# A two-layer encoder step on one core: full-row stick-breaking scores, value turn and late evictions moved, small moves in the down projection

## The chip, the core and the metric

One NeuronCore of a Trainium2 chip runs the whole program as one launch. The metric is the device time of one execution in microseconds (us). The engines work side by side, each with its own queue of instructions, and wait for each other by semaphores: TensorE (PE; its weight loads are shown as PEld), VectorE (DVE), ScalarE (ACT), GpSimd (POOL), and SyncE (SP), which issues most of the DMAs.

## The reference, cut to what matters

One inference step of a trunk with two layers for two requests at once: a prompt of 512 tokens and a sample of 64 tokens that has 512 cached keys. Layer 0 mixes tokens by attention with forget gates, layer 1 by stick-breaking attention; both have 12 heads of 64 and, beside them, 4 heads that read 256 memory tokens.

```python
def sb_block(q, k, v, qpos, kpos):
    z = jnp.einsum('bqhd,bkhd->bhqk', q.astype(jnp.float32), k.astype(jnp.float32)) * SCALE
    mask = kpos[None, :] < qpos[:, None]
    u = jnp.where(mask, jax.nn.log_sigmoid(-z), 0.0)
    rest = lax.cumsum(u, axis=3, reverse=True) - u
    a = jnp.where(mask, jnp.exp(jax.nn.log_sigmoid(z) + rest), 0.0)
    return jnp.einsum('bhqk,bkhd->bqhd', a.astype(v.dtype), v)
...
    x = x + o @ w_out
    gate, up = jnp.split(rmsnorm(x, g_ffn) @ w_gate_up, 2, axis=-1)
    return x + (jax.nn.silu(gate) * up) @ w_down
```

D_MODEL is 1024, D_FF 2816. Everything is fp32.

## The kernel before

Activations lie with features on the 128 partitions and the 576 tokens (64 of the sample, then 512 of the prompt) along the free axis. A large product is made of three products in a faster fp32 format: each operand is split into a high half (made by ACT) and a low half (the rest, by VectorE or GpSimd), and high x high, high x low and low x high are added (`passes`, L692). A weight tile of 512 KB is loaded by SP (`slab`, L428), gets its high half from ACT (`high`, L1010) and its low half from GpSimd (`low`, L567), and is then used by TensorE in eight pieces of six matmuls.

Attention goes by calls: two memory calls and six pair calls (two heads each) in each layer (`calls`). A call has nine units: for each of four blocks of 128 queries one for each head (units 0 to 7), and unit 8 for the sample's 64 queries of both heads. TensorE's order in a call is written out by hand in `attention` (L851): in every unit some pieces of the input projection for a later pair (`fill`, shared out by `spread`), the transposes of the unit before (`turn`, into the PSUM bank `turned`, from which ACT copies), and the scores of a unit further on. The products with the values of the call before stand in unit 0 (`values`, prompt) and unit 3 (`values_sample`). The value tile of the call's own pair is turned in unit 1, between two pieces (L884). In the last call the pieces are those of the output projection.

ACT and VectorE run the same units in their own `attention` (L1149, L1466). A forgetting unit goes VectorE (`front`), ACT (exponential), VectorE (`normalize`); a stick-breaking unit goes ACT (`softplus`, three activations), VectorE (`front`: a sum, a reversed scan, a difference), ACT (exponential). Between, ACT copies what was turned, makes the high halves of the finished outputs (`out_high`) and of a weight tile; VectorE makes their low halves (`out_low`, tile `o_lo`) and takes finished projections out of PSUM (`fill_out`). `out_ps`, one PSUM bank, is free again for the late sample product only when `out_low(prev, 0)` is done.

In `scores_one` (L774) a stick score contracts the 64 rows of one head: head 0 on partitions 0 to 63, head 1 on 64 to 127, and the mask is added by a product of 128 rows after it. The sample scores (L785) contract all 128 rows, with queries that are zero in the other head's rows.

The down projection (`down`, L959) makes each pair of output tiles from seven products (a scheme with block sums) in three chunks of the hidden features. Per product ACT makes the weight's high half (`d_high`) and, for five of seven, a copy of the weight in PSUM; VectorE makes the low half from the copy, or from SBUF where there is none (`d_copy`, `d_low`), and adds the product to x. In a layer's last chunk ACT also splits the new x (`split_new`), VectorE makes x's low half in layer 0, GpSimd adds the squares.

Of the kernel before, what the change touches and what calls it, by code (L numbers as in the profile page):

```python
# [99 lines left out]
def build(nc, x_t, mem_t, w_mkv, w_in, w_f, w_out, w_gu, w_dn, gains, b_f, ck, cv, clf, cmk, cmv,  # L100
# [4 lines left out]
    def sb(name, shape, dt=F32, stack=ctx):  # L105
# [40 lines left out]

    gates = at("gates", [P, 2, 2, SEQ])
    ckb = [gates[:, i] for i in range(2)]
    ckbs_cum = at("ckbs_cum", [P, 2 * KEYS_S])
    ckbs = [ckbs_cum[:, i * KEYS_S:(i + 1) * KEYS_S] for i in range(2)]  # L150
# [14 lines left out]
    m_lo = [sb("m_lo", [P, KT, N_MEM], F32R, region)[:, :, :],  # L165
            gates[:, :, :, :].bitcast(F32R).rearrange("p a b (k c) -> p (a b k) c", c=N_MEM)]
    region.close()
# [126 lines left out]
    class Call:  # L294
# [4 lines left out]

        def __init__(self, layer, half, par, mem=False, tiles=(), spread=(0,) * UNITS, fill=0):  # L300
            self.layer, self.par, self.mem = layer, par, mem
            self.a = a = half * 2 + par
            self.last = isinstance(a, int) and a == ATTNS - 1
            self.stick = layer == 1 and not mem
            self.pair = None if mem else a - MEM_PAIRS
            self.o_tile = PAIRS + a if mem else a - MEM_PAIRS
            self.unit = (a + layer * ATTNS) * UNITS
            self.use = attn_use(layer, a)
            start = 2 * DEPTH + layer * LAYER_ROUNDS
            self.round = a * MEM_ROUNDS + start if mem else \  # L310
                a * PAIR_ROUNDS + (start + MEM_PAIRS * (MEM_ROUNDS - PAIR_ROUNDS))
            self.out = (a + layer * ATTNS) * 2
            self.qkv = layer * IN_TILES + a + 1 if mem else a * 3 + (layer * IN_TILES - 1)
            self.qk = self.qkv if mem else self.qkv - 1
            self.caches = (half + (layer * ATTNS // 2 + 1)) * 32
            self.cums = half * 64
            self.tiles = tiles
            self.slabs = [fill * 6 + (layer_slab(layer) + t) for t, _ in tiles]
            self.nums = [fill * 6 + (layer_tile(layer) + t) for t, _ in tiles]
            self.spread = spread  # L320

            beside = [u for u, n in enumerate(spread) for _ in range(n)]
            self.per = len(beside) // len(tiles) if tiles else 0
            self.starts = [beside[self.per * n] for n in range(len(tiles))] if beside else []
            self.ends = [beside[self.per * n + self.per - 1] for n in range(len(tiles))] if beside else []
# [32 lines left out]
    def calls(eng, layer, call):  # L358
# [4 lines left out]
        def pair(half, par, t, fill=0):  # L363
            return Call(layer, half, par, False, [(t + c, "qkv"[c]) for c in range(3)],
                        (2, 2, 2, 3, 3, 3, 3, 3, 3) if layer else (1, 3, 3, 3, 2, 3, 2, 3, 4), fill)

# [3 lines left out]
        last = Call(layer, ATTNS // 2 - 1, 1, False, [(IN_TILES, "o"), (IN_TILES + 1, "o")],  # L370
                    (0, 1, 2, 1, 1, 0, 0, 1, 1) + (1,) * 7)
        call(mem0, None, mem1)
# [36 lines left out]
    def d_copy(pair, p):  # L409

        n = pair * PRODUCTS + p % PRODUCTS
        return acc[:, n // 2 % 2, n % 2, :] if p >= RING and p % PRODUCTS not in (1, 4) else None

# [152 lines left out]
    def _(pool):  # L566
# [16 lines left out]
        def zero_rows(layer):  # L583


            tiles = [vf_z[:, 0:DEC]]
            for par in range(2):
                tiles += [qs[par][HD:P, 0:DEC], qs[par][0:HD, DEC:]]
            for n, tile in enumerate(tiles):
                pool.memset(tile, 0.0).then_inc(zeroed, 1)  # L590
                pool.wait_ge(zeroed, len(tiles) * layer + n + 1)

# [98 lines left out]
    def _(pe):  # L691
# [82 lines left out]
        def scores_one(c, u):  # L774

            i, hd = divmod(u, 2)
            if u == 0:
                pe.wait_ge(qkv_ready, c.qk)
            pe.wait_ge(score_free, c.use + u - 1)
            rows, out = slice(hd * HD, (hd + 1) * HD), score[:, c.buf(u), 0:c.width(u)]  # L780
            pe.matmul(out, q[c.par][rows, DEC + i * P:DEC + (i + 1) * P], kb[c.par][rows, KEYS_S:KEYS_S + c.width(u)],  # L781
                      start=True, stop=False)
            mask_on(c, u, out).then_inc(score_ready, 1)
# [67 lines left out]
        def attention(c, prev, nxt):  # L851
# [24 lines left out]
            for u in range(UNITS):  # L876
                pieces = c.spread[u]
                half = pieces // 2
                fill(pieces - half)
                if u == 0 and prev is not None:  # L880
                    turn(prev, 2 * QT)
                    values(prev)
                    turn_rest(prev)
                if u == 1 and not c.mem:  # L884
                    pe.wait_ge(qkv_ready, c.qkv)
                    turn_blocks(c.round, vf[:, DEC:], QT)
                if u == 3 and prev is not None:
                    values_sample(prev)
                fill(half)
                if u:  # L890
# [29 lines left out]
        for layer in range(DEPTH):  # L920
# [19 lines left out]
            product(s0 + 1, t0 + 1, 1, 1, xg_hi, xg_lo)  # L940
            pe.wait_ge(zeroed, 5 * (layer + 1))
            pe.wait_ge(masks_made, 1)
# [66 lines left out]
    def _(act):  # L1009
# [139 lines left out]
        def attention(c, prev, nxt):  # L1149
            if prev is None and c.stick:  # L1150
                softplus(c, 0)
            for u in range(UNITS):
# [7 lines left out]
                if u == 1 and prev is not None:  # L1160
                    out_high(prev, 0)
                if u == 1 and not c.mem:
                    copy_round(c.round, v[c.par][:, :, :], turned[:, :].rearrange("p (j c) -> p j c", j=QT))
                if u:
                    copy_turned(c, u - 1)
                if u == 4 and prev is not None:
                    out_high(prev, 1)
# [18 lines left out]
        for layer in range(DEPTH):  # L1186
# [83 lines left out]
            for chunk, count in enumerate(CHUNKS):  # L1270
# [9 lines left out]
                for p in range(CHUNK_PRODUCTS):  # L1280
                    if p + RING < CHUNK_PRODUCTS:
                        d_high(chunk, p + RING)
                    if p < 3:
                        tail_high(chunk, p + 2)
                    if p == PRODUCTS and (chunk < len(CHUNKS) - 1 or layer < DEPTH - 1):
                        high(sg + 2 * (CHUNK0[chunk] + count) + 1, 1)
                    m, r = divmod(p, PRODUCTS)
                    if chunk == len(CHUNKS) - 1:
                        if r == 6:
                            split_new(2 * m)  # L1290
                        elif r == 0 and m:
                            split_new(2 * m - 1)
# [6 lines left out]
    def _(dve):  # L1299
# [62 lines left out]

        def queries(slab, tpar, par, scale):
            dve.wait_ge(slab_done, slab + 1)
            for hd in range(2):
                rows, cols = slice(hd * HD, (hd + 1) * HD), slice(hd * DEC, (hd + 1) * DEC)
                dve.scalar_tensor_tensor(out=qs[par][rows, cols], in0=acc[rows, tpar, 0, 0:DEC], scalar=scale,
                                         in1=rstd[rows, 0:DEC], op0=ALU.mult, op1=ALU.mult)
            return tile_out(slab, tpar, [(q[par], slice(0, P), scale)])

# [63 lines left out]
        def fill_out(c, n):  # L1434
# [3 lines left out]
            if what == "q":  # L1438
                last = queries(slab, t % 2, par, -SCALE if c.layer == 0 else SCALE)
            elif what == "k":  # L1440
# [12 lines left out]
        def attention(c, prev, nxt):  # L1453
            if prev is None:
                front(c, 0)
            for u in range(UNITS):
# [8 lines left out]
                if not c.stick and not early:  # L1465
                    normalize(c, u)  # L1466
                if u in (2, 5) and prev is not None:
                    out_low(prev, u // 5)
                if u in c.ends and c.tiles[0][1] != "o":
# [260 lines left out]
```

## Time and profile before

| | us |
|---|---|
| median of 3 runs (1481.46 to 1485.0) | 1483.07 |
| profiled execution | 1484.24 |
| its span | 1482.5 |
| granted TensorE clock, mean | 0.994 |
| PE busy | 1421.3 (96%) |
| DVE busy | 852.0 (57%) |
| ACT busy | 684.6 (46%) |
| POOL busy | 528.7 (36%) |

Busy time is the time in which an engine has an instruction under way; for TensorE it holds overlaps and ends that are modelled. Of the chain of work that ended last, 86% is TensorE's, 6% ACT's, 5% VectorE's. The times of the rows below are us from the start of the span.

### The profile page before, as it was taken

Reading aid. Unit: us, or ns where it says so; the run is one execution under the profiler, and the core shown is the slowest. Engines: PE = TensorE matmul, PEld = TensorE weight load, DVE = VectorE, ACT = ScalarE, POOL = GpSimd, SP = SyncE. Lnnn points to the kernel's source line nnn. Section 1 sums busy time; section 2 is a strip of 40 time slices with the busy share of each in tenths; the row PEclk is TensorE's granted clock in tenths of the full one; section 3 lists DMA queues with packets and bytes.
Section 4 is the critical chain, followed back from the end, with each engine's and each line's share of the span. In section 5 each row is a group of like instructions: output and inputs, shape, how many; then the busy total and the mean of one; then the engine's idle time right before and its main releaser. Section 6 shows DMA issues by size and latency. Waiting matters only on the chain.

```text
span 1482.5 us, 25893 instructions
## 1 busy us (share of the span) xinstructions
PE 1421.3 (96%) x10248; PEld 1321.6 (89%) x10248; DVE 852.0 (57%) x1376; ACT 684.6 (46%) x1287; POOL 528.7 (36%) x291
## 2 busy tenths in 40 slices
PE   6899999899999999999899999989999999999995
PEld 5778888699999999999887777758999999999995
DVE  6655555424574566456755655663257555755575
ACT  5454444533362236224745667674424422532364
POOL 2511212064433354334632111113534334433444
PEclk9999999999999999999999999999999999999998
DMA  6233333122322232223222222211223223222222
GB/s 260 74 95 126 117 110 111 41 75 86 115 71 72 85 106 79 71 85 107 64 72 88 76 77 81 74 45 44 85 86 97 75 85 113 72 72 85 99 59 92
DMA packets 49438, 130.69 MB, mean 88 GB/s; under 512 B 5532, under 2 KB 11676, under 8 KB 49216
## 3 DMA queue, kind: packets, MB, share of 16 engines
q1 hardware_dynamic: 44688, 121.23, 24.7%
q10 hardware_dynamic: 4656, 8.21, 1.5%
q8 instruction: 58, 0.95, 0.3%
q14 instruction: 36, 0.29, 0.1%
HBM read 118.85 MB, written 10.57 MB: 87 GB/s over the span
## 4 chain that ended last, share of the span: by engine, by line
PE 86%; ACT 6%; DVE 5%; issue 1%; DVEq 0%; DMA 0%; ACTq 0%; POOL 0%; SPq 0%; POOLq 0%
PE acc L699 60%; PE score L983 8%; PE out_ps L983 4%; PE turned L804 3%; PE out_ps L833 2%; PE score L781 2%; PE turned L983 2%; PE score L766 1%; ACT w_hi L1019 1%; DVE d_lo L1578 1%; PE out_ps L844 1%; PE score L793 1%; PE score L754 1%; DVE work_b L1416 1%; ACT work_c L1043 0%
## 5 line engine op out<-in xcount | busy, mean ns | idle before, releaser
L571 POOL TENSOR_TENSOR w_lo<-w_raw,w_hi 128x1024 fp32r<-128x1024 f32 x142 | 344.7, 2428 | 673.2 <-ACT w_hi L1019 651.9
L699 PE MATMUL acc<-xg_hi,w_hi 128*128 128x288 f32 x2048 | 452.1, 302 | 0.8 <-POOL w_lo L571 0.8
L699 PE MATMUL acc<-xg_hi,w_lo 128*128 128x288 f32 x2048 | 438.3, 296 | 0.0
L699 PE MATMUL acc<-xg_lo,w_hi 128*128 128x288 f32 x2048 | 438.0, 295 | 0.0
L699 PEld LDWEIGHTS acc<-xg_hi,w_hi 128*128 128x128 f32 x2048 | 327.8, 189 | 8.7 <-issue 7.1
L699 PEld LDWEIGHTS acc<-xg_hi,w_lo 128*128 128x128 f32 x2048 | 329.5, 188 | 0.0
L699 PEld LDWEIGHTS acc<-xg_lo,w_hi 128*128 128x128 f32 x2048 | 329.2, 188 | 0.0
L1019 ACT ACTIVATE w_hi<-w_raw 128x1024 fp32r<-128x1024 f32 x146 | 154.4, 1058 | 363.7 <-PE acc L699 356.5
L1531 DVE TENSOR_TENSOR work_b<-work_b,rstd 128x576 f32<-128x576 f32 x44 | 94.4, 2146 | 39.5 <-ACT work_b L1221 39.5
L983 PE MATMUL score<-f_hi,d_hi 128*128 128x288 f32 x352 | 105.0, 298 | 6.9 <-DVE x L1587 6.8
L1118 ACT ACTIVATE pt<-turned 128x256 f32<-128x256 f32 (+3 forms) x128 | 53.8, 420 | 115.7 <-PE turned L804 114.6
L983 PE MATMUL score<-f_lo,d_hi 128*128 128x288 f32 x352 | 103.8, 295 | 0.0
L983 PE MATMUL score<-f_hi,d_lo 128*128 128x288 f32 x352 | 103.7, 295 | 0.0
L580 POOL TENSOR_TENSOR sumsq<-sumsq,work_c 128x576 f32<-128x576 f32 x34 | 50.7, 1491 | 127.9 <-ACT work_c L1043 127.6
L1557 DVE TENSOR_TENSOR f_lo<-f_new,f_hi 128x576 fp32r<-128x576 f32 (+1 forms) x38 | 73.2, 1925 | 40.2 <-ACT f_hi L1232 40.2
L1578 DVE TENSOR_TENSOR d_lo<-acc,d_hi 128x512 fp32r<-128x512 f32 (+1 forms) x108 | 69.5, 644 | 40.5 <-ACT d_hi L1257 40.2
L804 PE MATMUL turned<-cst,work_b 128*128 128x128 f32 x372 | 68.3, 278 | 13.2 <-ACT vs L1118 5.3
L1357 DVE TENSOR_TENSOR work_a<-acc,rstd 128x576 f32<-128x576 f32 x44 | 33.2, 755 | 75.5 <-PE acc L699 62.1
L1545 DVE TENSOR_TENSOR f_new<-acc,work_b 128x576 f32<-128x576 f32 x38 | 28.8, 757 | 82.4 <-PE acc L699 82.4
L983 PEld LDWEIGHTS score<-f_hi,d_hi 128*128 128x128 f32 x352 | 66.0, 187 | 9.6 <-DVE d_lo L1578 7.6
L1383 DVE SCALAR_TENSOR_TENSOR work_a<-score,work_c 128x512 f32<-128x512 f32 (+3 forms) x54 | 27.7, 514 | 69.7 <-ACT work_c L1104 67.0
L804 PEld LDWEIGHTS turned<-cst,work_b 128*128 128x128 f32 x372 | 46.5, 141 | 22.3 <-issue 11.2
(181 smaller groups left out, 2429.8 us busy)
## 6 DMA issues: line engine op xcount, KB each, us to landing
w_raw<-in_w_gu SPq DMA_DIRECT2D x88, 512.0 KB, 3.4
w_raw<-in_w_in SPq DMA_DIRECT2D x40, 512.0 KB, 3.5
w_raw<-in_w_out SPq DMA_DIRECT2D x16, 512.0 KB, 3.5
d_raw<-in_w_dn SPq DMA_DIRECT2D x16, 512.0 KB, 3.7
d_raw<-in_w_dn SPq DMA_DIRECT2D x32, 256.0 KB, 2.7
out_k_o<-kb ACTq DMA_DIRECT2D x12, 288.0 KB, 2.5
out_v_o<-vf_z ACTq DMA_DIRECT2D x12, 288.0 KB, 3.2
kb<-in_ck SPq DMA_DIRECT2D x12, 256.0 KB, 2.6
```

The source lines that it names most:

```text
L571: pool.tensor_tensor(w_lo[par][:, 0:cols], raw(s, par, cols), w_hi[par][:, 0:cols].bitcast(F32), ALU.subtract).then_inc(wlo_made, 1)
L580: pool.tensor_tensor(sumsq[:, :], sumsq[:, :], work_c[:, m % 2, :], ALU.add) \
L699: mm = pe.matmul(acc[:, tpar, h, 0:c1 - c0], w[par][:, k * P:(k + 1) * P], a[:, c0:c1], start=first and n == 0, stop=last and n == 2)
L781: pe.matmul(out, q[c.par][rows, DEC + i * P:DEC + (i + 1) * P], kb[c.par][rows, KEYS_S:KEYS_S + c.width(u)], start=True, stop=False)
L804: mm = pe.transpose(turned[:, j * P:(j + 1) * P], tile[:, j * P:(j + 1) * P], ident)
L983: mm = pe.matmul(bank, w, a[:, f, k, :], start=(k == 0 and q == 0 and r in (0, 1, 3)), stop=(k == kts - 1 and q == 2), skip_group_check=True)
L1019: act.activation(w_hi[par][:, 0:cols], raw(s, par, cols), ACT.Copy).then_inc(whi_made, 1)
L1118: act.activation(out, src, ACT.Copy).then_inc(turned_free, 1)
L1357: last = dve.tensor_tensor(halves(out), src, halves(rstd[rows, :]), ALU.mult)
L1531: dve.tensor_tensor(work_b[:, 0, :], work_b[:, 0, :], rstd[:, :], ALU.mult)
L1557: dve.tensor_tensor(f_lo[:, own, i, :], src, f_hi[:, own, i, :].bitcast(F32), ALU.subtract) .then_inc(flo_made, 1)
L1578: dve.tensor_tensor(d_lo[:, n % RING, 0:cols], whole[:, 0:cols], d_hi[:, n % RING, 0:cols].bitcast(F32), ALU.subtract).then_inc(dlo_made, 1)
```

## The change

- `scores_one` reads queries from a new tile `qz`: for each head 128 rows, of which the other head's 64 are zero; the matmul takes all 128 rows of the keys. In layer 1 `queries` writes each head's 64 rows there, in two instructions, in place of the one to `q`; four memsets on GpSimd at the start of layer 1 zero the rest. `qz` lies where the forget gates lay; the low half of the second layer's memory tile gets a name of its own at the same place.
- The value tile is turned in unit 0, after that unit's pieces, in place of unit 1; ACT's copy of it moves likewise.
- In pair calls other than the last, all pieces of units 1 to 8 come before the late sample product and the turn. In layer 0 one piece moves from unit 8 to unit 0.
- In the last call the late sample product moves from unit 3 to 2, its `out_high` from 4 to 2, the two `out_low` from units 2 and 5 to 1 and 3.
- In the down projection the high half of the weight tile that follows a chunk moves four products later; half of the splits of x move two products later; in layer 0's last chunk, behind the first pair, the two products without a PSUM copy are 2 and 5 in place of 1 and 4.

```diff
+    early = ExitStack()
+    m_lo1 = sb("m_lo1", [P, KT, N_MEM], F32R, early)
+    early.close()
+    gate_room = at("gate_room", [P, 2 * 2 * SEQ + 2 * KEYS_S])
+    qz = gate_room[:, 0:2 * 2 * TOK].rearrange("p (a b c) -> p a b c", a=2, b=2)
...
+            self.late = (2, 2, 1, 3) if last else (3, 4, 2, 5)
...
-                        (2, 2, 2, 3, 3, 3, 3, 3, 3) if layer else (1, 3, 3, 3, 2, 3, 2, 3, 4), fill)
+                        (2, 2, 2, 3, 3, 3, 3, 3, 3) if layer else (2, 3, 3, 3, 2, 3, 2, 3, 3), fill)
...
-        return acc[:, n // 2 % 2, n % 2, :] if p >= RING and p % PRODUCTS not in (1, 4) else None
+        beside_x = pair // OUT_PAIRS == len(CHUNKS) - 1 and p > PRODUCTS
+        return acc[:, n // 2 % 2, n % 2, :] if p >= RING and p % PRODUCTS not in ((2, 5) if beside_x else (1, 4)) else None
...
                 tiles += [qs[par][HD:P, 0:DEC], qs[par][0:HD, DEC:]]
+                if layer:
+                    tiles += [qz[HD:P, par, 0, :], qz[0:HD, par, 1, :]]
...
-            rows, out = slice(hd * HD, (hd + 1) * HD), score[:, c.buf(u), 0:c.width(u)]
-            pe.matmul(out, q[c.par][rows, DEC + i * P:DEC + (i + 1) * P], kb[c.par][rows, KEYS_S:KEYS_S + c.width(u)],
+            out = score[:, c.buf(u), 0:c.width(u)]
+            pe.matmul(out, qz[:, c.par, hd, DEC + i * P:DEC + (i + 1) * P], kb[c.par][:, KEYS_S:KEYS_S + c.width(u)],
...
-                half = pieces // 2
+                half = pieces // 2 if u == 0 or c.last or c.mem else 0
                 fill(pieces - half)
...
-                if u == 1 and not c.mem:
+                if prev is not None and u == c.late[0]:
+                    values_sample(prev)
+                fill(half)
+                if u == 0 and not c.mem:
                     pe.wait_ge(qkv_ready, c.qkv)
                     turn_blocks(c.round, vf[:, DEC:], QT)
-                if u == 3 and prev is not None:
-                    values_sample(prev)
-                fill(half)
...
-            pe.wait_ge(zeroed, 5 * (layer + 1))
+            pe.wait_ge(zeroed, (5, 14)[layer])
...
-                if u == 1 and not c.mem:
+                if u == 0 and not c.mem:
                     copy_round(c.round, v[c.par][:, :, :], turned[:, :].rearrange("p (j c) -> p j c", j=QT))
...
-                if u == 4 and prev is not None:
+                if prev is not None and u == c.late[1]:
                     out_high(prev, 1)
...
-                    if p == PRODUCTS and (chunk < len(CHUNKS) - 1 or layer < DEPTH - 1):
+                    if p == PRODUCTS + 4 and (chunk < len(CHUNKS) - 1 or layer < DEPTH - 1):
                         high(sg + 2 * (CHUNK0[chunk] + count) + 1, 1)
...
-                        elif r == 0 and m:
+                        elif r == 2 and m:
                             split_new(2 * m - 1)
...
+            if stick:
+                return tile_out(slab, tpar, [(qz[hd * HD:(hd + 1) * HD, par, hd, :], slice(hd * HD, (hd + 1) * HD), scale)
+                                             for hd in range(2)])
...
-                if u in (2, 5) and prev is not None:
-                    out_low(prev, u // 5)
+                if prev is not None and u in c.late[2:]:
+                    out_low(prev, c.late[2:].index(u))
```

## Rows read from the trace of the kernel before

**Rows 1.** The page, busy us, share of the span and instructions of each engine.
```profile
PE 1421.3 (96%) x10248; PEld 1321.6 (89%) x10248; DVE 852.0 (57%) x1376; ACT 684.6 (46%) x1287; POOL 528.7 (36%) x291
```

**Rows 2.** Busy us by stretch: stretch, length, each engine, PEclk, DMA share, GB/s.
```profile
198.79:230.22 31.43, 31.43 (x230) 26.76 (x229) 17.51 (x47) 13.98 (x36) 7.16 (x3) 1.00 0.36 113
904.36:939.91 35.55, 34.92 (x230) 27.91 (x229) 21.29 (x37) 24.87 (x56) 7.18 (x3) 1.00 0.22 77
...
995.00:1000.00 5.00, 3.06 (x8) 1.64 (x8) 4.52 (x8) 2.95 (x6) 0.00 (x0) 0.50 0.00 0
```

**Rows 3.** Waits of PE from 760 to 1013: us in total, times, longest.
```profile
PE turned L804 <- ACT vs L1118: 4.5, 6, 1.4
...
PE out_ps L844 <- DVE o_lo L1424: 1.8, 2, 1.0
```

**Rows 4.** Order of time, PE, a 64-row stick score: start, us, what, count.
```profile
886.81 0.38 PE L804 MATMUL turned<-cst,work_b 128*128 128x128 f32 x2
887.12 1.12 PE L781 MATMUL score<-kb,qb 64*128 64x512 f32 x2
...
888.56 0.42 PE L699 MATMUL acc<-xg_lo,w_hi 128*128 128x288 f32 x2
```

**Rows 5.** Order of time, PE, the 128-row sample score of the same call.
```profile
894.67 0.49 PE L804 MATMUL turned<-cst,work_b 128*128 128x128 f32 x3
...
895.86 0.33 PE L793 MATMUL out_ps<-kb,qs 128*128 128x64 f32 x2
896.03 0.19 PE L754 MATMUL out_ps<-mask_b,ident_b 128*128 128x64 bf16 x1
...
896.41 0.43 PE L699 MATMUL acc<-xg_lo,w_hi 128*128 128x288 f32 x2
```

**Rows 6.** Order of time, PEld, the weight loads of that sample score.
```profile
894.89 0.30 PEld L793 LDWEIGHTS score<-kb,qs 128*128 128x128 f32 x2
```

**Rows 7.** Order of time, ACT, units 0 and 1 of a stick-breaking pair call.
```profile
907.20 1.05 ACT L1019 ACTIVATE w_hi<-w_raw 128x1024 fp32r<-128x1024 f32 x1
...
910.55 0.59 ACT L1118 ACTIVATE vs<-turned 128x512 f32<-128x512 f32 x1
```

**Rows 8.** Order of time, PE, unit 3 of that call.
```profile
916.19 0.42 PE L699 MATMUL acc<-xg_lo,w_hi 128*128 128x288 f32 x2
916.45 0.43 PE L699 MATMUL acc<-xg_hi,w_lo 128*128 128x288 f32 x2
916.73 1.13 PE L844 MATMUL out_ps<-pts,vcs 128*128 128x128 f32 x8
```

**Rows 9.** Order of time, DVE, the end of the sample unit of that call.
```profile
937.36 0.21 DVE L1390 TENSOR_TENSOR work_a<-out_ps,work_c 128x64 f32<-128x64 f32 x1
```

**Rows 10.** Order of time, PE, unit 6 of layer 1's last call; idle before in brackets.
```profile
997.86 2.05 PE L793 MATMUL score<-kb,qs 128*128 128x512 f32 x2 [1.74 <-DVE o_lo L1430]
```

**Rows 11.** Order of time, PE, unit 3 of layer 0's last call.
```profile
272.38 1.13 PE L844 MATMUL out_ps<-pts,vcs 128*128 128x128 f32 x8 [1.18 <-DVE o_lo L1424]
```

**Rows 12.** Order of time, PE, the fifth product in both layers' last chunk.
```profile
715.88 0.37 PE L983 MATMUL score<-f_hi,d_hi 128*128 128x288 f32 x1 [1.82 <-DVE x L1587]
728.27 0.37 PE L983 MATMUL score<-f_hi,d_hi 128*128 128x288 f32 x1 [0.96 <-DVE x L1587]
...
1450.03 0.37 PE L983 MATMUL score<-f_hi,d_hi 128*128 128x288 f32 x1 [0.87 <-DVE x L1587]
```

**Rows 13.** Order of time, ACT, before the first of these waits.
```profile
711.04 1.04 ACT L1019 ACTIVATE w_hi<-w_raw 128x1024 fp32r<-128x1024 f32 x1
```

**Rows 14.** Line L1578, low halves read from SBUF: ns min/median/max, first and last start, forms.
```profile
L1578 DVE TENSOR_TENSOR d_lo<-d_sum,d_hi x54: 542/681/1955, 403.3 to 1459.0; 128x512 fp32r<-128x512 f32 x36, 128x384 fp32r<-128x384 f32 x18
```

**Rows 15.** Order of time, DVE, a pair's queries.
```profile
919.89 0.76 DVE L1359 SCALAR_TENSOR_TENSOR qb<-acc,rstd 128x576 f32<-128x576 f32 x1
```

**Rows 16.** Order of time, POOL, the start of layer 1.
```profile
749.61 0.75 POOL L590 MEMSET qs<- 64x64 f32 x4
753.53 2.41 POOL L571 TENSOR_TENSOR w_lo<-w_raw,w_hi 128x1024 fp32r<-128x1024 f32 x1 [3.17 <-ACT w_hi L1019]
```

More of the change, by code:

```diff
@@ L145, in build @@
     pts = at("pts", [P, QT * P + P])
-    gates = at("gates", [P, 2, 2, SEQ])
+    early = ExitStack()
+    m_lo1 = sb("m_lo1", [P, KT, N_MEM], F32R, early)
+    early.close()
+    gate_room = at("gate_room", [P, 2 * 2 * SEQ + 2 * KEYS_S])
+    gates = gate_room[:, 0:2 * 2 * SEQ].rearrange("p (a b c) -> p a b c", a=2, b=2)
     ckb = [gates[:, i] for i in range(2)]
-    ckbs_cum = at("ckbs_cum", [P, 2 * KEYS_S])
+    ckbs_cum = gate_room[:, 2 * 2 * SEQ:]
+    qz = gate_room[:, 0:2 * 2 * TOK].rearrange("p (a b c) -> p a b c", a=2, b=2)
     ckbs = [ckbs_cum[:, i * KEYS_S:(i + 1) * KEYS_S] for i in range(2)]
@@ L165, in build @@
     m_lo = [sb("m_lo", [P, KT, N_MEM], F32R, region)[:, :, :],
-            gates[:, :, :, :].bitcast(F32R).rearrange("p a b (k c) -> p (a b k) c", c=N_MEM)]
+            m_lo1[:, :, :]]
     region.close()
@@ L294, in build, with __init__ @@
     class Call:
-        def __init__(self, layer, half, par, mem=False, tiles=(), spread=(0,) * UNITS, fill=0):
+        def __init__(self, layer, half, par, mem=False, tiles=(), spread=(0,) * UNITS, fill=0, last=False):
             self.layer, self.par, self.mem = layer, par, mem
@@ L370, in calls @@
         last = Call(layer, ATTNS // 2 - 1, 1, False, [(IN_TILES, "o"), (IN_TILES + 1, "o")],
-                    (0, 1, 2, 1, 1, 0, 0, 1, 1) + (1,) * 7)
+                    (0, 1, 2, 1, 1, 0, 0, 1, 1) + (1,) * 7, last=True)
         call(mem0, None, mem1)
@@ L588, in zero_rows @@
                 tiles += [qs[par][HD:P, 0:DEC], qs[par][0:HD, DEC:]]
+                if layer:
+                    tiles += [qz[HD:P, par, 0, :], qz[0:HD, par, 1, :]]
             for n, tile in enumerate(tiles):
                 pool.memset(tile, 0.0).then_inc(zeroed, 1)
-                pool.wait_ge(zeroed, len(tiles) * layer + n + 1)
+                pool.wait_ge(zeroed, 5 * layer + n + 1)
         for n in range(2):
@@ L1361, in tile_out, with queries @@
             return last
-        def queries(slab, tpar, par, scale):
+        def queries(slab, tpar, par, scale, stick=False):
             dve.wait_ge(slab_done, slab + 1)
+            if stick:
+                dve.wait_ge(zeroed, 14)
             for hd in range(2):
@@ L1368, in queries @@
                                          in1=rstd[rows, 0:DEC], op0=ALU.mult, op1=ALU.mult)
+            if stick:
+                return tile_out(slab, tpar, [(qz[hd * HD:(hd + 1) * HD, par, hd, :], slice(hd * HD, (hd + 1) * HD), scale)
+                                             for hd in range(2)])
             return tile_out(slab, tpar, [(q[par], slice(0, P), scale)])
@@ L1438, in fill_out @@
             if what == "q":
-                last = queries(slab, t % 2, par, -SCALE if c.layer == 0 else SCALE)
+                last = queries(slab, t % 2, par, -SCALE if c.layer == 0 else SCALE, c.layer == 1)
             elif what == "k":
```

## The prediction

> **What bounds the kernel now.** I read the page first: TensorE is busy 96% of the span [rows 1]. Then the busy times call by call. A call of layer 0 is full of TensorE work, 31.43 of 31.43 us; a stick-breaking call of layer 1 takes 35.55 with 34.92 busy, while ACT works 24.87 and VectorE 21.29 [rows 2]. So TensorE's queue is the bound, and a change pays by taking time out of it or by removing a wait in it. The waits of TensorE in layer 1 say which there are: on ACT's copy of the turned value tile (`vs`, 4.5 us in six waits, the longest 1.4 in the last call, so 0.62 in each of the other five) and on VectorE's `o_lo` (1.8 in two, 0.8 and 1.0) [rows 3]. "Busy" also hides something, which only the order of time shows: next part.
>
> **The scores.** Take a 512-column stick score, 64 rows deep. The transposes before it end at 886.81 + 0.38 = 887.19, and the input projection runs evenly again from 888.56: 1.37 us [rows 4]. The sample score of the same call does the same with 128 rows: transposes end at 895.16, even running from 896.41, 1.25 us, and in it are 0.17 of a second small product (896.03 - 895.86) and a mask narrower by 64 columns, about 0.03 [rows 5]. Without them 1.11. The two 512-column products themselves are not faster or slower by rows; the difference is at the two ends, where TensorE goes from full to half rows and back. Price: 0.26 us a score. There are 6 pairs x 8 = 48 of them: 2 beside the second memory call, 8 beside each of five pair calls, 6 in the last. That is 12.5 us of TensorE's queue, at most.
>
> The weights of the 128-row score begin to load at 894.89, while the transposes still run [rows 6]. The Trainium skill, "TensorE: Matmul & The Clock Gate", The mechanism, says that a weight load overlaps a running matmul only where the row groups differ; full-row scores would then pay for their loads. The row says otherwise, so I give that rule a small chance as a rival below.
>
> **Value turn, u = 1 to u = 0.** The five waits of 0.62 go, since the copy of the value tile is now a unit ahead of the turn that waits for it. What is late next is ACT. Before, ACT did a weight copy (1.05) and went straight to the softplus of unit 2; the value copy (0.59) came a unit later [rows 7]. Now the value copy waits for the value turn behind TensorE's second piece, the weight copy comes after it, and softplus 2 starts some 1.1 us later, while TensorE comes earlier. From it hang unit 2's and 3's VectorE work and then `o_lo`, for which the late sample product waits: now it starts at 916.73 with one piece (0.79: three pairs of matmuls, 0.26 apart) still to come [rows 8]. ACT reaches softplus 3 about when it does now (what it has to do before that is the same, in another order), so `o_lo` and that product come about where they are, at 916.6 by my count, but with the piece done: 0.9 us won, where 3 scores and the value wait would be worth 1.4. I book 0.6 handed back (with the little wait there). At the end of a call the next call's second score needs the buffer that VectorE frees when the sample unit is done, at 937.57 [rows 9]; TensorE comes to it only a little after that, and by one or two scores (0.26 to 0.52) sooner after the change: 0.2 handed back. The call that waited 0.8 for `o_lo` loses that too, as all three pieces now come before.
> Five pair calls: 5 x (8 x 0.26 + 0.62) + 0.8 - 5 x 0.8 = 10.3.
>
> **Last calls.** In layer 1 it is a chain, not a queue: ACT, VectorE and TensorE wait for each other, and the sample scores start at 997.86 after 1.74 of idling [rows 10]. Following ACT's order: the value turn first costs a wait of half a us, as no piece covers it; its 1.4 wait goes; the sample product a unit earlier lets VectorE's `o_lo` out of the way before unit 6. I get the sample scores at about 995.8, 2.0 earlier, with the second memory call's two scores (0.5, of which 0.2 handed back) 2.3. TensorE is granted half its clock there (0.50, the 1.2 GHz level, in 995 to 1000, in which it is busy 3.06 of 5.00) [rows 2]; I leave that as it is. In layer 0 the last call waits 1.18 for `o_lo` [rows 11]; the same move takes that wait, lets the units behind it start sooner, and delays one pair of scores by a us: 1.5 gained.
>
> **Layer 0's other calls.** No wait to remove, and one more piece at u = 0, one less at u = 8, are the same pieces. Value: 0, bounds -1.5 to +1.5.
>
> **Down projection.** In each layer's last chunk TensorE stands before the fifth product of a pair: 1.82, 0.96, 0.96 in layer 0, 0.42 and 0.87 in layer 1, together 5.0 [rows 12]. ACT is the cause: it does x's split, and in layer 0's second pair a weight copy of 1.04 too, before the high half that this product needs [rows 13]. The change puts the copy four products later and the split two; both fit between other high halves there. What may be late next is VectorE: the low halves that are read from SBUF alone move to the two products beside which x's low half is made, and such a low half takes 0.68 alone and up to 1.96 [rows 14]. I take 4.0 of the 5.0, bounds 2.5 and 5.0. The Trainium skill, "SBUF — State Buffer", Who interferes with whom, has VectorE with two SBUF inputs shut out for a whole GpSimd instruction; by it a pair could give back another us, 3 less in all.
>
> **What is added.** Two half-height products for the padded query in place of one: 0.76 more on VectorE for each pair [rows 15], 4.6 in all, hidden by its 14 us of idling in a call [rows 2]; uncovered it would cost those 4.6. Four memsets of 576 columns on GpSimd: no row; from 0.2 each (as those of 64 columns, 0.19 apart) to 1.8 (in proportion), I take 0.2, the nearest row. GpSimd idles 3.17 before its next weight half [rows 16]; even 7.2 in all would delay that half (from 753.53, 2.41 long) by 4.0, to 760.0, when TensorE needs it. SP's cache loads are released by the late sample product, now 0.7 later within its unit in most calls; the weight tile queued behind them is copied three units (11 us) later. Nothing.
>
> **Sum.** 10.3 + 2.3 + 1.5 + 4.0 = 18.1. The profiled execution took 1484.24 (span 1482.5); 1484.2 - 18.1 = 1466.1. The median of the runs is 1.2 below the profiled one: 1465.0.
>
> **Rivals.**
> - *ACT hands most of it back.* If softplus 2's lateness runs through the whole call, a pair call gains 1.0 instead of 2.1, the last ones 1.5 together, the down projection 2.5: 9.0, so 1474. For it: ACT is without slack around units 0 and 1; against: 10.7 us of idling in a call [rows 2].
> - *Nothing is handed back.* 14.3 in the pair calls, 0.5 beside the memory call, the last calls 4.5 and 3.0 (the clock stays up), down 5.0: 27.3, so 1456. Against it is ACT's order, worked out above.
> - *The padding does nothing*, because the time at the ends belongs to the mask or the scores themselves: only waits go, 3.9 + 1.0 + 1.5 + 4.0 = 10.4, 1473. Against it: [rows 4, 5].
> - *Full-row loads are not hidden* (the skill's rule above): two loads of 0.19 against 0.26 saved, 48 x 0.12 = 5.8 lost, other gains 10.4: 1478. Against it: [rows 6].
> - *Slower.* The call starts become the bound in both layers: softplus 2 later by the weight copy (1.05) in six calls, layer 0's second pair of scores later by a piece and the turn (1.3) in six, nothing won on the scores: 6.3 + 7.8 - 4.0 in the down projection, 1493. It decides only where the chain from those scores has less than 1.3 us in hand when its turn is due; layer 0's calls show no wait at all [rows 2].
>
> **Chances.** Forecast 0.56, most handed back 0.18, nothing handed back 0.13, padding does nothing 0.06, loads 0.02, slower 0.05. About 0.2% (3 us) can be told from no change. Faster: all but the last, less 0.03 for a first rival that hands back the rest as well: 0.92; same 0.03; slower 0.05. Range 1457 to 1475: it leaves out the far ends of the second and the last rival.
>
> **What would show it.** After an L781 score no gap of its load, and even running 1.1 us after the transposes; the line `turned <- ACT vs` gone from TensorE's waits; pair calls of about 33.5; the softplus of unit 2 later against its score; the last chunk's waits before the fifth product below 0.4. Wrong if pair calls stay above 34.5, or if TensorE shows new waits on ACT's copies at u = 0 or 1 in layer 0.

## The result and the profile after

The changed kernel takes 1461.73 us (median of 4 runs, 1461.07 to 1461.87) against 1483.53 for the kernel before, timed beside it: ratio 0.985, 95% interval 0.9838 to 0.9863. Forecast were 1465.0, and 1457 to 1475 as the range. The time fell into the range; of the terms of the sum the largest came out over a third larger than forecast, and another less than half of its forecast. The profiled execution took 1461.77 (span 1460.0), 22.5 less than that of before.

TensorE's busy time fell by 15.3 us and its share stayed [rows 1]:

```profile
PE 1406.0 (96%) x10248; PEld 1322.6 (91%) x10248; DVE 857.3 (59%) x1382; ACT 681.4 (47%) x1287; POOL 529.4 (36%) x295
```

A call is measured from its first matmul with the values to that of the next call. Busy times of the calls that answer to [rows 2], of layer 1's last call, and of the stretch in it with the low clock (stretch, length, PE, PEld, DVE, ACT, POOL, PEclk, DMA share, GB/s):

```profile
198.19:229.46 31.27, 31.27 (x231) 26.73 (x230) 17.51 (x47) 13.98 (x36) 7.16 (x3) 1.00 0.34 113
889.25:922.03 32.78, 32.66 (x230) 28.22 (x229) 21.60 (x38) 24.23 (x56) 7.19 (x3) 1.00 0.24 83
954.82:987.51 32.69, 24.69 (x140) 17.84 (x139) 17.99 (x30) 21.44 (x49) 2.37 (x1) 0.90 0.10 35
972.82:978.82 6.00, 4.63 (x9) 2.02 (x10) 4.24 (x6) 4.17 (x8) 0.00 (x0) 0.54 0.00 1
```

The pair call of layer 1 went from 35.55 to 32.78, and one of layer 0, which was to stay, lost 0.16. All calls put against those of before give this table (us, read from the two traces; the row of the down projections holds all that lies behind a layer's last call):

| term of the sum | forecast | measured |
|---|---|---|
| five pair calls of layer 1 | 10.3 | 14.3 |
| second memory call's two scores and layer 1's last call | 2.3 | 0.9 (0.17 + 0.76) |
| layer 0's last call | 1.5 | 1.3 |
| layer 0's other calls | 0 | 0.7 (four by 0.17) |
| down projections | 4.0 | 5.0 (3.5 + 1.5) |
| before the first call | – | 0.3 |
| sum | 18.1 | 22.5 |

The sum was 4.4 too small: 6.0 too little in four rows, of which 1.6 too much in the two rows of the last calls hid a part. That the total came as near as it did is in so far luck.

**The scores** did what was forecast. The same stretch as in [rows 4], first TensorE, then its weight load:

```profile
909.10 0.49 PE L816 MATMUL turned<-cst,work_b 128*128 128x128 f32 x3
909.43 1.02 PE L793 MATMUL score<-kb,gate_room 128*128 128x512 f32 x2
910.29 0.22 PE L766 MATMUL score<-mask_b,ident_b 128*128 128x128 bf16 x1
...
910.67 0.42 PE L711 MATMUL acc<-xg_lo,w_hi 128*128 128x288 f32 x2
```

```profile
909.32 0.30 PEld L793 LDWEIGHTS score<-kb,gate_room 128*128 128x128 f32 x2
909.86 0.10 PEld L766 LDWEIGHTS score<-mask_b,ident_b 128*128 128x128 bf16 x1 [0.24 <-issue]
```

From the end of the transposes (909.10 + 0.49 = 909.59) to even running (910.67) are 1.08 us; 1.37 before. The load of the full-row score begins at 909.32, inside the transposes.

**ACT, units 0 and 1**, the rows that answer to [rows 7], with the softplus of units 2 (894.58) and 3 (896.82):

```profile
893.14 0.60 ACT L1130 ACTIVATE vs<-turned 128x512 f32<-128x512 f32 x1 [0.95 <-PE turned L816]
893.63 1.05 ACT L1031 ACTIVATE w_hi<-w_raw 128x1024 fp32r<-128x1024 f32 x1
894.58 0.37 ACT L1111 ACTIVATE work_c<-score 128x256 f32<-128x256 f32 x1
...
896.82 0.39 ACT L1111 ACTIVATE work_c<-score 128x256 f32<-128x256 f32 x1
```

Softplus 2 is late, as forecast: its score was complete at 893.6, 1 us before. From 850 to 954, three pair calls but for the last 0.8 us, TensorE's waits have no line any more; in those 0.8 us the last pair call has a wait of 0.70 on ACT (at 954.26). The order of time shows what that view leaves out, here VectorE's front of unit 2 and then TensorE:

```profile
897.29 0.42 DVE L1407 TENSOR_TENSOR work_a<-score,work_c 128x256 f32<-128x256 f32 x1
```

```profile
897.42 0.27 PE L816 MATMUL turned<-cst,work_b 128*128 128x128 f32 x1
897.82 0.91 PE L793 MATMUL score<-kb,gate_room 128*128 128x384 f32 x2
...
901.06 0.94 PE L856 MATMUL out_ps<-pts,vcs 128*128 128x128 f32 x7
```

The score of unit 4 starts when that front has freed its buffer, 0.40 behind the transpose's start, in place of 0.11 where nothing is waited for (run 5 below). The late sample product at 901.06 waits for nothing.

**Layer 1's last call** (954.82 to 987.51) now waits in other places:

```profile
PE score L793 <- DVEq L1409: 2.6, 2, 1.3
PE turned L816 <- ACT pt L1130: 2.1, 2, 1.2
PE out_ps L856 <- DVE o_lo L1441: 1.8, 1, 1.8
PE score L805 <- DVEq L1409: 1.1, 1, 1.1
PE turned L816 <- ACT pts L1130: 0.5, 1, 0.5
```

### The profile page after: what moved, and what is told of

It reads as the page before. It is cut to its first block, busy times and chain, and to the rows that moved or that the text cites. A ratio compares the mean times of both kernels' runs of the same rounds, so it can differ in the third digit from the quotient of the medians.

```text
span 1460.0 us, 25909 instructions
## 1 busy us (share of the span) xinstructions
PE 1406.0 (96%) x10248; PEld 1322.6 (91%) x10248; DVE 857.3 (59%) x1382; ACT 681.4 (47%) x1287; POOL 529.4 (36%) x295
## 4 chain that ended last, share of the span: by engine, by line
PE 88%; DVE 5%; ACT 4%; issue 1%; DVEq 1%; DMA 0%; POOL 0%; ACTq 0%; SPq 0%; POOLq 0%
PE acc L711 60%; PE score L995 9%; PE out_ps L995 4%; PE turned L816 3%; PE out_ps L845 2%; PE turned L995 2%; PE score L778 2%; PE score L793 1%; ACT w_hi L1031 1%; PE score L805 1%; PE out_ps L856 1%; DVE work_c L1403 1%; DVE work_b L1433 1%; PE score L766 0%; DMA m_raw<-in_mem_t 0%
## 5 line engine op out<-in xcount | busy, mean ns | idle before, releaser
L590 POOL TENSOR_TENSOR sumsq<-sumsq,work_c 128x576 f32<-128x576 f32 x34 | 50.2, 1475 | 134.5 <-ACT work_c L1055 134.4
L1433 DVE TENSOR_SCALAR work_b<-work_b,inv 128x256 f32<-128x256 f32 (+4 forms) x90 | 62.3, 693 | 8.1 <-issue 0.9
L995 PEld LDWEIGHTS score<-f_hi,d_lo 128*128 128x128 f32 x352 | 66.2, 188 | 0.0
```

Of the source, the lines that this page charges most:

```text
L590: pool.tensor_tensor(sumsq[:, :], sumsq[:, :], work_c[:, m % 2, :], ALU.add) \
L995: mm = pe.matmul(bank, w, a[:, f, k, :], start=(k == 0 and q == 0 and r in (0, 1, 3)), stop=(k == kts - 1 and q == 2), skip_group_check=True)
L1433: dve.tensor_scalar(work_b[:, b, 0:w], work_b[:, b, 0:w], inv[:, b:b + 1], None, ALU.mult).then_inc(probs_ready, 1)
```

## Experiments

Nine kernels; the first four were timed together, the next four too, the last by itself, each time beside the kernel before (1483.33, 1483.79, 1482.74). The ratio is to the kernel before. Runs 5 and 6 lie 1.7 us below the changed kernel, and their intervals overlap with its own; what they tell rests on the traces.

| | median us | ratio, 95% interval |
|---|---|---|
| scores on 64 rows again | 1471.70 | 0.9918 (0.9904 to 0.9932) |
| value turn back | 1467.50 | 0.9892 (0.9876 to 0.9908) |
| down projection back | 1467.27 | 0.9894 (0.9878 to 0.9909) |
| before, padding alone | 1476.02 | 0.9950 (0.9936 to 0.9964) |
| weight copy first | 1460.03 | 0.9836 (0.9823 to 0.9850) |
| last call: value turn at unit 1 | 1460.06 | 0.9836 (0.9822 to 0.9849) |
| last call rearranged | 1458.09 | 0.9823 (0.9809 to 0.9836) |
| weight first and last call | 1455.78 | 0.9810 (0.9796 to 0.9823) |
| the same, scores on 64 rows | 1468.48 | 0.9899 (0.9876 to 0.9923) |

**1. Scores on 64 rows again.**

```diff
-            pe.matmul(out, qz[:, c.par, hd, ...], kb[c.par][:, ...],
+            pe.matmul(out, qz[rows, c.par, hd, ...], kb[c.par][rows, ...],
```

> The changed kernel with one thing undone: a stick-breaking score reads the 64 rows of its own head again instead of all 128 (the zero halves are still written, but not read). Theory A (a 64-row score between 128-row matmuls costs TensorE's queue 0.26 us, 48 times, and nothing of it is handed back): 12.5 us more, 1474.2, a pair call of layer 1 2.1 longer (34.9 instead of 32.8). Rival B (ACT or VectorE takes back a part, as forecast: about 0.8 of 2.1 in a call): 1470, a pair call 34.1. Rival C (the padding does nothing, the gain came from the waits and the order): 1461.7.

10.0 more, a pair call 34.64. The same stretch, and the call:

```profile
915.98 0.49 PE L816 MATMUL turned<-cst,work_b 128*128 128x128 f32 x3
916.40 1.12 PE L793 MATMUL score<-kb,gate_room 64*128 64x512 f32 x2
917.45 0.23 PE L766 MATMUL score<-mask_b,ident_b 128*128 128x128 bf16 x1
...
917.84 0.42 PE L711 MATMUL acc<-xg_lo,w_hi 128*128 128x288 f32 x2
```

```profile
895.00:929.64 34.64, 34.64 (x230) 27.88 (x229) 21.71 (x38) 24.54 (x56) 7.22 (x3) 1.00 0.23 79
```

From 916.47 (915.98 + 0.49) to 917.84 are 1.37 again, with nothing changed but the rows: rival C falls. A call loses 1.86, between A and B: something is handed back in the changed kernel, but not 0.8. And the moves alone, without the padding, are worth 35.55 - 34.64 = 0.91 a call, where the wait that they removed was read as 0.62.

The weight loads show where the price of a score lies:

```profile
916.40 0.29 PEld L793 LDWEIGHTS score<-kb,gate_room 64*128 64x128 f32 x2 [0.17 <-issue]
917.45 0.10 PEld L766 LDWEIGHTS score<-mask_b,ident_b 128*128 128x128 bf16 x1 [0.76 <-issue]
```

Between products that all take 128 rows a load begins under the product before: in the changed kernel 0.11 ahead of its score (909.32 for 909.43) and 0.43 ahead of its mask (909.86 for 910.29). Where the rows change it begins only with its own product, here at 916.40 and 917.45, and so in all 48 scores of this run. From start to start this makes 0.09 more before the score, 0.10 more in the first of its two passes (the x2), 0.09 more before the mask and 0.01 behind it: 0.30 a score, at 128 columns as at 512. Whether the load itself or something that holds it up takes the time, the records do not tell.

**2. Value turn back at unit 1.**

```diff
-                half = pieces // 2 if u == 0 or c.last or c.mem else 0
+                half = pieces // 2
...
-                if u == 0 and not c.mem:
+                if u == 1 and not c.mem:
                     pe.wait_ge(qkv_ready, c.qkv)
                     turn_blocks(c.round, vf[:, DEC:], QT)
...
```

> The changed kernel with the value turn back at unit 1, on TensorE and ACT, and the pieces of the input projection in their old places. Theory A (the move is worth the waits that it took away: 0.62 in each of five pair calls of layer 1, up to 1.0 in its last call, 0.17 in four calls of layer 0, and the wait of 0.8 for o_lo): 3.8 to 5.6 more, 1465.5 to 1467.3, and the line of waits on ACT's vs is there again. Rival B (ACT's lateness at softplus 2 handed back what the wait gave, as forecast 0.6 in a call): about 1 more, 1462.7. Rival C (with the scores shorter the chain behind the turn decides, so the wait grows by what the scores gave): 8 or more, 1470.

5.8 more. Waits of TensorE over three pair calls (850 to 961), then a pair call and layer 1's last call:

```profile
PE turned L816 <- ACT vs L1130: 1.9, 3, 0.6
PE out_ps L856 <- DVE o_lo L1441: 1.4, 3, 0.5
```

```profile
893.84:927.75 33.91, 32.83 (x231) 28.22 (x230) 21.59 (x38) 24.48 (x56) 7.18 (x3) 1.00 0.24 80
961.66:993.33 31.67, 25.58 (x140) 19.06 (x139) 17.96 (x30) 21.54 (x49) 2.38 (x1) 0.84 0.10 36
```

A pair call takes 1.13 more, theory A by place, with a wait on top that A did not have: `o_lo` is now late in every call. Layer 0's calls are back at 31.43, so the 0.17 there belong to this move, with the pieces that go along with it. Layer 1's last call, against all theories, is 1.0 *shorter* than in the changed kernel: there the move costs.

**3. Down projection back.**

```diff
-        beside_x = pair // OUT_PAIRS == len(CHUNKS) - 1 and p > PRODUCTS
+        beside_x = False
...
-                    if p == PRODUCTS + 4 and (chunk ...
+                    if p == PRODUCTS and (chunk ...
...
-                        elif r == 2 and m:
+                        elif r == 0 and m:
```

> The changed kernel with the three moves in the down projection undone. Theory A (the five waits before the fifth product were all of it, and VectorE's low halves cost nothing in their new place): 5.0 more, 1466.7. Rival B (a fifth to a half of it is handed back by the low halves that are now made beside x's): 2.5 to 4.0 more, 1464.2 to 1465.7, and waits of TensorE for them in the changed kernel that are gone here.

5.5 more by the runs, 5.0 by the traces (3.7 in layer 0, 1.4 in layer 1). TensorE's waits for x in layer 0's last chunk, here and then in the changed kernel:

```profile
PE score L995 <- DVE x L1604: 3.9, 4, 1.8
```

```profile
PE score L995 <- DVE x L1604: 0.5, 1, 0.5
```

Theory A but for one wait: a fifth product is waited for no more, and the one wait that is left in the changed kernel, 0.45, is rival B's. TensorE comes to a third product that waits for VectorE's sum, which stands behind a low half of 1.42 beside GpSimd:

```profile
717.36 1.80 POOL L662 TENSOR_TENSOR d_sum<-d_raw 128x512 f32<-128x512 f32 x1 [1.06 <-DVE d_lo L1595]
718.29 1.42 DVE L1595 TENSOR_TENSOR d_lo<-d_sum,d_hi 128x512 fp32r<-128x512 f32 x1
720.22 0.37 PE L995 MATMUL score<-f_hi,d_hi 128*128 128x288 f32 x1 [0.45 <-DVE x L1604]
```

The longest of the low halves read from SBUF is now 1.43 where [rows 14] has 1.96. Which of the three moves took which wait was not tried.

**4. The kernel before with the padding alone** (the changed kernel with the edits of runs 2 and 3 together, and `late` at (3, 4, 2, 5) in every call).

> The kernel before with the padded queries alone: value turn, late evictions, pieces and down projection as before. Theory A (the padding is worth 0.26 on the queue at each of 48 scores whatever else is done): 12.5 less than the 1483.5 of before, 1471.0, and the waits on vs and o_lo stay as they are. Rival B (without the moves the chain over ACT and VectorE keeps its time, so TensorE comes earlier to the same waits: vs and o_lo grow by about 0.8 in a call): 8.5 less, 1475. Rival C: the padding does nothing, 1483.

7.3 less: rival B, and more of it than B said. A pair call takes 33.92 in place of 35.55, 1.63 less. Waits over three pair calls (850 to 960):

```profile
PE turned L816 <- ACT vs L1130: 1.9, 3, 0.6
PE out_ps L856 <- DVE o_lo L1441: 1.4, 3, 0.5
```

The wait on `vs` did not grow; the one on `o_lo`, which [rows 3] have in one of these three calls, is now in all three. So the padding by itself does hand back some 0.6 a call, at the place that the prediction named, and the value turn's move takes that away again.

**5. Weight copy first.** In unit 0 ACT makes the weight's high half (`weight` holds the lines that stood further down) before the copy of the value tile, not after it.

```diff
+                if u == 0 and u in c.starts:
+                    weight()
                 if u == 0 and not c.mem:
                     copy_round(c.round, v[c.par]...
...
-                if u in c.starts:
+                if u and u in c.starts:
```

> The changed kernel with ACT's order at unit 0 of a call turned round: first the weight copy, which waits for nothing, and then the copy of the value tile, for which ACT now stands 0.95 us. Theory A (what a pair call of layer 1 hands back is ACT's lateness at the softplus of unit 2: TensorE's score of unit 4 starts 0.38 late, behind VectorE's front of unit 2, in each call): softplus 2 starts 0.9 sooner, the 0.38 goes in five calls, a pair call 32.4, the time 1459.8. Rival B (that wait hangs on something else, VectorE's own queue for one): 32.8 and 1461.7. Rival C (the value copy, 0.6 later, is now late for TensorE's turn of unit 0): new waits on vs, 1463 or more.

1.7 less than the changed kernel. ACT, then TensorE at the score of unit 4, and the call:

```profile
891.14 1.06 ACT L1031 ACTIVATE w_hi<-w_raw 128x1024 fp32r<-128x1024 f32 x1
892.19 0.60 ACT L1130 ACTIVATE vs<-turned 128x512 f32<-128x512 f32 x1
892.68 0.38 ACT L1111 ACTIVATE work_c<-score 128x256 f32<-128x256 f32 x1
```

```profile
896.47 0.27 PE L816 MATMUL turned<-cst,work_b 128*128 128x128 f32 x1
896.58 0.81 PE L793 MATMUL score<-kb,gate_room 128*128 128x384 f32 x2
```

```profile
888.30:920.71 32.41, 32.41 (x230) 28.21 (x229) 21.60 (x38) 24.40 (x56) 7.18 (x3) 1.00 0.24 84
```

Theory A, in place and size: ACT's 0.95 of idling is filled, softplus 2 starts 4.38 into the call in place of 5.33, the score follows its transpose by 0.11, the call is 0.37 shorter. What a pair call handed back was ACT's lateness, and it was 0.37.

**6. Value turn at unit 1 in layer 1's last call alone.**

```diff
+            self.turn_at = 1 if last and layer else 0
...
-                if u == 0 and not c.mem:
+                if u == c.turn_at and not c.mem:
```

> The changed kernel with the value turn back at unit 1 in the last call of layer 1 alone. Theory A (in that call the forecast 2.0 failed because the value turn at unit 0, which no piece covers, holds up ACT and so o_lo, and the sample product waits 1.75 for it): the 1.75 goes, 1.4 on vs comes back, the chain behind it starts 1.0 sooner; the last call 31.7 instead of 32.7, the time 1460.7. Rival B (the end of that call hangs on VectorE's and ACT's chain alone, whatever the turn does): 32.7, 1461.7.

1.7 less. The last call, and in it the turn that waits on `vs` and the late sample product:

```profile
955.19:985.73 30.54, 23.27 (x141) 17.82 (x140) 17.98 (x30) 21.67 (x49) 2.37 (x1) 0.94 0.11 38
```

```profile
961.02 0.30 PE L817 MATMUL turned<-cst,work_b 128*128 128x128 f32 x1 [1.43 <-ACT vs L1134]
...
962.60 1.05 PE L857 MATMUL out_ps<-pts,vcs 128*128 128x128 f32 x8
...
976.23 1.10 PE L806 MATMUL score<-kb,qs 128*128 128x512 f32 x2 [1.95 <-DVEq L1413]
```

Theory A: the 1.75 on `o_lo` is gone, 1.43 on `vs` is back, and the sample scores start 21.04 into the call in place of 22.07 (976.89 - 954.82). The trace shows 2.15 less, not 1.0: the call is, instruction for instruction, that of run 2, where it took 31.67 with its sample scores at the same 21.05; the 1.1 between them lie behind that point. There the granted clock differs (the call's mean is 0.94 here and 0.84 in run 2): the first two passes of the sample score, to the next product, took 0.93 here (976.23 to 977.16) and 1.84 in run 2 (982.71 to 984.55), at the 1.2 GHz level.

**7. Layer 1's last call rearranged.**

```diff
+            self.late = (3, 3, 1, 4) if last and layer else (2, 2, 1, 3) if last else (3, 4, 2, 5)
+            if last and layer:
+                self.starts = [5] + self.starts[1:]
...
-                    (0, 1, 2, 1, 1, 0, 0, 1, 1) + (1,) * 7, last=True)
+                    ((0, 1, 1, 1, 1, 1, 1, 1, 0) if layer else (0, 1, 2, 1, 1, 0, 0, 1, 1)) + (1,) * 7, last=True)
```

> As the run with the value turn back at unit 1 in layer 1's last call, and in that call besides: the late sample product back at unit 3 with its o_lo still made at unit 1 and 4, the output projection's pieces one each at units 1 to 7 (units 5 and 6, where TensorE waits 1.3, get one each), and the weight copy at unit 5 instead of unit 1, out of the way of the softplus of unit 3. Theory A (the call is one chain of score, softplus and VectorE's front, two buffers deep, and it runs as early as its first links: score 4 comes 1.7 sooner, softplus 3 0.8 sooner): the last call 29.5 to 30, the time 1458.5 to 1459. Rival B (the links behind it, on VectorE 2.8 and on ACT 3.1 a unit, set the pace from the start): 31.7, 1460.7. Rival C (the sample product at unit 3 delays the later scores instead): over 32.7, over 1461.7.

3.6 less than the changed kernel, the call 29.27. Theory A: the score of unit 4 starts 7.52 into the call and the sample scores 19.57, so what comes early in that chain keeps most of its lead to the end. How the gain is shared between the sample product, the pieces and the weight copy was not tried.

**8. Weight copy first and the rearranged last call.**

> The weight copy first at unit 0 and the rearranged last call of layer 1 together. If both hold: 1461.7 less 1.9 less 2.7 to 3.2, 1456.6 to 1457.1; if only the weight copy holds 1459.8, if only the last call 1458.7.

5.9 less than the changed kernel; its interval to the kernel before (0.9796 to 0.9823) lies wholly below that of the changed kernel, so it beats both. By the traces 1.9 of it lie in the five pair calls and 3.6 in the last call. Its last call, with the score of unit 4 and the sample scores (the changed kernel has them 10.46 and 22.07 into the call, here 7.52 and 19.58):

```profile
952.47:981.54 29.07, 21.89 (x140) 16.50 (x139) 17.98 (x30) 21.32 (x49) 2.36 (x1) 1.00 0.11 39
```

```profile
959.99 0.81 PE L796 MATMUL score<-kb,gate_room 128*128 128x384 f32 x2
...
972.05 1.10 PE L808 MATMUL score<-kb,qs 128*128 128x512 f32 x2 [1.65 <-DVEq L1419]
```

**9. The same with the scores on 64 rows** (edit of run 1).

> The run with the weight copy first and the rearranged last call, with one thing undone: the scores read 64 rows again. It tells what a 64-row score costs where nothing is handed back. Theory A (0.30 us a score, as from the transposes before it to the projection behind it in the traces, and the pair calls of that run have no wait left that could give some back): 8 x 0.30 = 2.4 a pair call, 34.8 instead of 32.4, 12 in five, 0.3 beside the memory call, 0 to 1.8 in the last, 1468.1 to 1470. Rival B (0.23 a score, what undoing it cost in the changed kernel, is the whole price): 34.3 a call, 1465.5 to 1467.

12.7 more than run 8 by the medians; a pair call 34.64, to the hundredth that of run 1:

```profile
895.14:929.78 34.64, 34.64 (x230) 27.88 (x229) 21.71 (x38) 24.86 (x56) 7.21 (x3) 1.00 0.23 79
```

So with 64 rows TensorE's queue sets the call whatever ACT's order, and with 128 rows and ACT in time it sets it at 32.41. The difference is 2.23 for eight scores: 0.28 each. Theory A, a little below its 2.4: of the 0.30 that the records give for a score, the last one of run 8's call gets back only 0.20, as its first pass still takes 0.20 where that of the other score of 128 columns takes 0.11.

## Why the prediction came out as it did

**The scores: right, price 0.28 for 0.26.** Eight scores were worth 2.23 a call (run 9 against run 8), 2.1 was forecast, and run 1's loads put the time at the two changes of rows, as forecast. The Trainium skill, "TensorEngine Tiling (Array Packing)", Key Properties, says that a change of tiling mode drains TensorE. It gives no price; the traces give one, 0.28 for a lone half-row product between full-row ones, and do not tell whether it is a drain. That loads of the same rows would not overlap ("TensorE: Matmul & The Clock Gate", The mechanism, of the Trainium skill) is not what the load at 909.32 shows. In these runs it is the loads at a change of rows that do not.

**The value turn: right in place, worth 0.91 for 0.62.** Run 1 has this move without the padding. TensorE's matmuls are recorded with modelled ends, and the next normally starts some 0.15 before such an end (916.73 before 916.45 + 0.43 in [rows 8]). A wait read as the gap behind that end is short by as much: the 0.62 were some 0.78. The rest, about 0.1, may come from pieces that are no longer split around other work; no run shows it. The same 0.15 hid a wait in layer 0, whose calls were read as 31.43 busy of 31.43 [rows 2]: four times 0.17. There the transpose that waits for the value copy started 0.28 behind the start of the product before it (205.13), and 0.14 in the changed kernel.

**What is handed back: the step that failed.** The prediction put it so: "ACT reaches softplus 3 about when it does now (what it has to do before that is the same, in another order)", and from this booked 0.6 at the late sample product and 0.2 at the call's end. The work was the same, the idling was not. Before, ACT stood idle between softplus 2 and softplus 3, twice:

```profile
911.73 0.28 ACT L1127 ACTIVATE vn<-turned 128x128 f32<-128x128 f32 x1 [0.59 <-PE turned L806]
...
912.61 0.39 ACT L1099 ACTIVATE work_c<-score 128x256 f32<-128x256 f32 x1 [0.43 <-PE score L754]
```

Now it comes later to that stretch and finds turns and scores ready; the rows of after have no idling in it. Softplus 3 starts 7.57 into the call (896.82 - 889.25) in place of 8.25 (912.61 - 904.36), `o_lo` is made in time, and the late sample product waits for nothing. The 0.6 are real where ACT's order is the old one: run 4 pays them. What the changed kernel pays instead is 0.37 at the score of unit 4, by the same lateness of softplus 2, one place earlier than looked for (run 5). The account of a pair call: 2.23 + 0.91 - 0.37 = 2.77, measured 35.55 - 32.78 = 2.77; forecast 2.70 - 0.8 = 1.9. All three terms are differences between lengths of the same call in these runs, so that they add up says no more than that runs 1 and 9, and runs 5 and 8, agree. Three of the five calls gain 2.74 to 2.77, one 3.71 with its old wait of 0.8 on top, and the last 2.33, since it now ends in a wait of 0.7 on ACT: 14.3 together. The rival "nothing is handed back" had this 14.3 too, but by luck, with too low a price and no handing back, and its 7.5 for the last calls were 2.1.

**Layer 1's last call: 2.0 forecast, 0.76 measured.** "I get the sample scores at about 995.8", that is 20.8 into the call; they came at 22.07, from 22.83. The half microsecond of waiting for the value turn was counted, but not what ACT makes of it: softplus 2 stands behind the value copy, and behind softplus 2 the `o_lo` for which the sample product, a unit earlier, waits 1.75. In a pair call one piece covers that turn, here nothing does. Run 6 takes the move back in this call alone and gets its sample scores at 21.04; run 8 shows with 19.58 how much the order was worth.

**Layer 0's last call and the down projection: right in place.** 1.3 for 1.5, and 5.0 for 4.0: the upper bound, though one low half does hand 0.45 back (run 3). By the rule of the Trainium skill, "SBUF — State Buffer", Who interferes with whom, a pair could have given back another us beside GpSimd. The trace agrees with the rule, at a smaller price: that low half took 1.42 where 0.68 is usual, and ended 0.55 behind the GpSimd instruction beside it (719.71 and 719.16). So ACT was not the whole cause of the old waits either. The low half in front of the wait of 1.82 [rows 12] took 1.49, and it too ended 0.55 behind a GpSimd instruction (713.40 + 1.42):

```profile
713.88 1.49 DVE L1578 TENSOR_TENSOR d_lo<-d_sum,d_hi 128x512 fp32r<-128x512 f32 x1 [1.65 <-ACT d_hi L1257]
```

Some 0.8 of that wait were this low half, by the 0.68 that one takes alone.

**What was costed at nothing** cost nothing. A pair's padded queries took VectorE 1.52 for 0.76 (903.60), and it idled 0.47 right behind them. A pair of 576-column memsets on GpSimd took 1.21, 0.6 each where 0.2 was taken, and the second pair ended (747.14) before its next weight half was due:

```profile
744.27 1.21 POOL L602 MEMSET gate_room<- 64x576 f32 x2
```

Of the other rivals, "ACT hands most of it back" fell with the pair calls (2.77 where it had 1.0), "the padding does nothing" and "full-row loads are not hidden" with run 1 and the load's row, "slower" with the calls of layer 0. Of the signs that were named, the pair call came to 32.78 for about 33.5, and one wait of 0.45 in the last chunk, before a third product, is above the 0.4.

## What to carry to other kernels

A lone product on half of the rows between full-row products costs TensorE time at both changes of rows (0.30 us here, from 128 to 512 columns, 0.28 of it won in a whole call) that no busy time shows; the weight load that begins only with its own product does show it. To price such a thing, compare two stretches from the last common instruction before to the even running behind. When work on a second engine is put in another order, count where that engine idles in either order, not only what it has to do; and fill its idling first with what waits for nothing (the weight copy ahead of the value copy, 0.37 a call). An order that pays where a piece of other work covers a wait can cost where none does: the last turn of a loop wants an order of its own.

## What was not expected of the hardware

The granted clock at the end of layer 1's attention is not settled by the instructions of that call. The last call of runs 2 and 6 is the same list of instructions, with a mean granted clock of 0.84 and 0.94 and a length of 31.67 and 30.54. That of runs 7 and 8 is the same list too, with 0.94 and 1.00 and 29.27 and 29.07. In the changed kernel the 1.2 GHz level lies at about 973.3 to 980.1 (0.62 of full speed in 972.82 to 974.82, 0.50 up to 978.82, 0.68 in the next 2 us), behind two waits of TensorE of 1.3 each that end at 970.28 and 973.12. Why one execution is granted more than another is open.
